# Keys, values and queries of layer B for two tiles at once, in three stages instead of five

## The reference

```
for layer in range(2):                                  # A = layer 0, B = layer 1
    shift/scale/gate rows = silu(c) @ ada_w[layer] + ada_b[layer]
    h = rmsnorm(x) * (1 + scale) + shift
    out = mla_mixer(h) if layer == 0 else band_mixer(h, k_all, v_all)
    x = x + gate_m * out
    x = x + gate_f * peer_ffn(rmsnorm-modulated x)
    if layer == 0:                                      # keys and values of layer B, from x after layer A
        k_new, v_new = h_kv @ w_kv ; k_new = rmsnorm per head(k_new)
# band_mixer: q = rmsnorm per head(h @ w_q); scores + relative bias, softmax, values; @ w_o
# peer_ffn: 8 heads choose 16 of 16384 experts for each row; for each chosen expert e:
#   a = gelu(h . u[e]);  y += softmax weight * a * v[e]        (u and v rows are 1024 floats)
```

## Time and profile before

| | |
|---|---|
| time, three runs | 4121.85, 4123.65, 4124.06 us |
| profiled execution: its own time, its span | 4123.38 us, 4121.6 us |
| mean granted clock of TensorE | 0.807 |
| busy: PE, DVE, POOL, ACT | 64%, 57%, 55%, 13% of the span |
| bytes moved | 1478 MB, mean 359 GB/s |
| of these by the gathers' queue q0, by SP's q1 | 1268 MB, 196 MB |

### The profile page before, as it was taken

How to read it: one execution, slowest core, us unless ns; L and a number is a source line. 1 busy time by engine, 2 the same in 40 slices (tenths; PEclk the granted TensorE clock), 3 DMA queues, 4 the chain that set the end, 5 groups by cost and what they waited for, 6 DMA issues and landing times.

```text
span 4121.6 us, 31777 instructions
## 1 busy us (share of the span) xinstructions
PE 2658.0 (64%) x9649; PEld 966.8 (23%) x9649; DVE 2330.6 (57%) x5876; ACT 527.1 (13%) x1288; POOL 2254.6 (55%) x2374
## 2 busy tenths in 40 slices
PE   6778664565554555555458567575656767676699
PEld 2344441221221112122112222132223211111122
DVE  2237687785676466556654655774576466544410
ACT  2244320111010101110011111011011100000000
POOL 1101436456666556565665555556566666666665
PEclk9889776777676786678679778777868899999999
DMA  9845988899999999999999999999999999999999
GB/s 344 306 162 167 306 269 324 303 340 371 381 395 390 387 412 380 386 363 415 390 390 381 401 379 352 387 365 392 406 408 403 371 361 356 370 371 369 377 373 341
DMA packets 480552, 1478.18 MB, mean 359 GB/s; under 512 B 59088, under 2 KB 132864, under 8 KB 479712
## 3 DMA queue, kind: packets, MB, share of 16 engines
q0 software_dynamic: 347792, 1268.25, 80.3%
q1 hardware_dynamic: 107008, 195.85, 12.9%
q10 hardware_dynamic: 25584, 12.06, 1.0%
HBM read 1448.97 MB, written 28.57 MB: 358 GB/s over the span
## 4 chain that ended last, share of the span: by engine, by line
DMA 28%; PE 19%; POOL 17%; DVE 14%; issue 13%; another core or an unknown queue 6%; ACT 2%; SPq 1%; ACTq 0%; DVEq 0%; POOLq 0%
DMA A<-in_uv,A 25%; POOL A L2049 9%; POOL A L2069 8%; PE P L997 8%; DVE A L1875 7%; PE P L939 2%; PE P L905 2%; PE P L715 1%; PE P L867 1%; PE P L652 1%; PE P L734 1%; DMA A<-in_w_oB 1%; DVE A L1761 1%; DVE A L1764 1%
## 5 line engine op out<-in xcount | busy, mean ns | idle before, releaser
L997 PE MATMUL P<-A 128*32 128x512 f32 x4608 | 1357.6, 819 | 1053.4 <-DMA A<-in_uv,A 909.8
L1875 DVE CUSTOM_DVE_ANT_0 A<-P,A 128x1024 f32<-128x1024 f32 x1052 | 1278.9, 1224 | 1048.3 <-DMA A<-in_uv,A 908.2
L2049 POOL DMA_INDIRECT A<-in_uv,A x1152 | 1112.4, 966 | 891.6 <-DVE A L1875 604.0
L2069 POOL DMA_INDIRECT A<-in_uv,A x1152 | 1096.6, 952 | 619.3 <-issue 295.2
L997 PEld LDWEIGHTS P<-A 128*32 128x32 f32 x4608 | 272.7, 133 | 1940.8 <-issue 1508.8
L1016 PE MATMUL P<-A 128*128 128x512 f32 (+1 forms) x480 | 230.6, 625 | 27.9 <-DMA A<-in_w_kv 18.6
L867 PE MATMUL P<-A 128*128 128x128 f32 (+2 forms) x832 | 150.7, 315 | 94.6 <-issue 48.8
L905 PE MATMUL P<-A 128*128 128x512 f32 (+1 forms) x320 | 171.1, 677 | 25.3 <-DMA A<-in_w_oB 17.6
L881 PE MATMUL P<-A 128*64 128x128 f32 (+2 forms) x832 | 137.6, 301 | 44.9 <-ACT A L1360 26.3
L854 PE MATMUL P<-A 96*64 96x320 f32 (+9 forms) x320 | 149.2, 575 | 18.9 <-issue 7.1
L867 PEld LDWEIGHTS P<-A 128*128 128x128 f32 (+2 forms) x832 | 119.4, 210 | 160.1 <-issue 112.6
(11 more groups left out here) (190 smaller groups left out, 2120.1 us busy)
## 6 DMA issues: line engine op xcount, KB each, us to landing
A<-in_ada_w POOLq DMA_DIRECT2D x28, 2048.0 KB, 10.9
A<-in_w_kv SPq DMA_DIRECT2D x80, 512.0 KB
A<-in_uv,A POOLq DMA_INDIRECT x2304
A<-in_w_oA SPq DMA_DIRECT2D x40, 512.0 KB
A<-in_w_q SPq DMA_DIRECT2D x40, 512.0 KB
A<-in_w_oB SPq DMA_DIRECT2D x40, 512.0 KB
A<-in_p_w_q SPq DMA_DIRECT2D x2, 4096.0 KB, 15.0
A<-in_p_w_q SPq DMA_DIRECT2D x8, 512.0 KB
```

The costliest lines, as they stand in the source:

```text
L997: ins = pe.matmul(Y[32 * j:32 * j + 32, b, :], spread[:, w:w + STRIDE], row[:, 512 * b:512 * b + 512], start=(m == 0), stop=(m == STRIDE - ...
L1875: dve.tensor_tensor_reduce(u_slot[b], row, u_slot[b], 1.0, 0.0, ALU.mult, ALU.add, dots[u % 2][:, j:j + 1]).then_inc(sem("dots_done"), 1)
L2049: pool.indirect_dma_start(u_slot[at % U_SLOTS], None, table, bass.IndirectOffsetOnAxis(ap=expert[u % 2][:, j:j + 1], axis=0)).then_inc(sem ...
L2069: pool.indirect_dma_start(row, None, table, bass.IndirectOffsetOnAxis(ap=expertT[u % 3][:, n:n + 1], axis=0)).then_inc(sem(name), 16)
```

## The change

- `MIDDLES = {3: (PT, 0), 5: (1, 2), 7: (3,)}`: the middle runs in stages 3, 5 and 7, for two tiles, two tiles and one. Stages 4 and 6 have none.
- A chunk of weights is multiplied with both tiles' rows before its slot is given back. Tile b uses banks 2b and 2b + 1, for all three products, so a product waits until the one before has been copied out.
- The ring has three chunks. Keys and queries share one pair of buffers; the second tile has `h` buffers of its own, one in place of a row buffer `hrow`, one in place of two bias strips.
- ACT copies keys and queries out of PSUM and squares them there; DVE scales the copies.
- PE pulls at m = 7 and 8 (turns of the two norms), four pieces at m = 9 to 12, 14 and 15, the turn of the keys at m = 13 and of the queries at m = 17; the attention from m = 19.
- SP writes keys and values in the midst of the queries' chunks, ahead of the 20th, since the queries need the keys' buffers.

```diff
+MIDDLES = {3: (PT, 0), 5: (1, 2), 7: (3,)}
...
-        mid_ring = [A[:, at:at + D] for at in (22560, 23584, 24608, 28448)]
-        vst = w_o[1]
-        kn_b, qn_b = A[:, 26144:27168], A[:, 27168:28192]
-        h_kv, h_q = oT, hT
+        first_ring = [A[:, at:at + D] for at in (22560, 23584, 24608, 28448)]
+        mid_ring = [A[:, 22560 + D * b:22560 + D * (b + 1)] for b in range(3)]
+        kn_b = qn_b = [A[:, 25632 + D * b:25632 + D * (b + 1)] for b in range(2)]
+        vst = [A[:, 27680 + D * b:27680 + D * (b + 1)] for b in range(2)]
+        h_kv, h_q = [oT, chunks(38688)], [hT, chunks(33568)]
...
-            return (m - 17) * 23 // 13 - (m - 18) * 23 // 13 if m >= 18 else 0
+            return (m - 18) * 23 // 12 - (m - 19) * 23 // 12 if m >= 19 else 0
...  SP, middle
+                def rows_stored():
+                    for b, t in enumerate(tiles):
+                        sp.wait_ge(sem("bk_normed"), done // 16 - len(tiles) + b + 1)
+                        load(o["bk_p"][rows_of(t), :] if t < PT else o["bk_s"][PAST - DEC:, :], kn_b[b][0:ROWS[t], :], "bk_stored")
+                    sp.wait_ge(sem("bv_copied"), i + 1)
+                    for b, t in enumerate(tiles):
...
+                sp.wait_ge(sem("out_chunks"), C * (stage + 2))
                 for x, (w, lo) in enumerate((("w_kv", 0), ("w_kv", D), ("w_q", 0))):
                     for c in range(C):
                         n = n0 + C * x + c
-                        if n - n0 >= 4:
-                            sp.wait_ge(sem("mid_chunks"), n - 3)
+                        if n - n0 >= 3:
+                            sp.wait_ge(sem("mid_chunks"), n - 2)
+                        if n - n0 == 19:
+                            rows_stored()
...  PE, middle
+                for b in range(2):
+                    if b < len(tiles):
+                        turn_norm("mid", tiles[b])
+                    yield
+                pe.wait_ge(sem("hT_ready"), norm_at["mid", tiles[-1]] + 1)
+                for x, (h, emptied) in enumerate(((h_kv, None), (h_kv, "bk_squared"), (h_q, "bkT_copied"))):
+                    if x == 2:
+                        turn_rows_back("bk", kn_b, "bv_copied", i)
+                        yield
+                    if emptied:
+                        pe.wait_ge(sem(emptied), i + 1)
                     for c in range(C):
                         n = n0 + C * x + c
+                        pe.wait_ge(sem(f"mid{n % 3}_loaded"), 16 * (C // 4 + n // 3 + 1))
+                        for b in range(len(tiles)):
+                            for half in range(2):
+                                ins = pe.matmul(P[:, 2 * b + half, :], h[b][:, c, :], mid_ring[n % 3][:, 512 * half:512 * half + 512],
+                                                start=(c == 0), stop=(c == C - 1), skip_group_check=True)
                         ins.then_inc(sem("mid_chunks"), 1)
                         yield
+                turn_rows_back("bq", qn_b, "bq_squared", i)
...  PE, the order of a stage
-                        if m in (7, 14, 16):
+                        if m in (7, 8, 13, 17):
                             pull(between)
-                        elif 8 <= m < 14:
+                        elif 9 <= m < 16:
                             pull(between, 4)
...  ACT
+                if u >= 2:
+                    act.wait_ge(sem("row_placed"), u - PLACED)
+                    act.wait_ge(sem("dots_done"), u_at(u - 1) + 4)
...
+            def middle_copies(i, x, rows, name):
+                tiles, squared = MIDDLES[list(MIDDLES)[i]], (xn, vst[1])
+                act.wait_ge(sem("mid_chunks"), 3 * C * i + (x + 1) * C)
+                for b in range(len(tiles)):
+                    for half in range(2):
+                        at = slice(512 * half, 512 * half + 512)
+                        ins = act.copy(rows[b][:, at], P[:, 2 * b + half, :])
+                        if name != "bv":
+                            ins = act.activation(squared[b][:, at], P[:, 2 * b + half, :], ACT.Square)
...
+                for name in ("bk_stored", "bv_stored", "vB_stored"):
+                    act.wait_ge(sem(name), 16 * done)
+                middle_copies(i, 2, qn_b, "bq")
...  DVE
+                for b in range(2):
+                    if b < n:
+                        if b == 0:
+                            dve.wait_ge(sem(f"{name}_rms"), i + 1)
+                            step(dve.reciprocal(stat[:, 64:64 + HEADS * n], stat[:, 64:64 + HEADS * n]))
+                        x = dst[b].rearrange("p (h e) -> p h e", h=HEADS)
+                        step(dve.tensor_tensor(x, x, bc(stat[:, 64 + HEADS * b:80 + HEADS * b].unsqueeze(2), [128, HEADS, BD]), ALU.mult))
+                        dve.tensor_tensor(x, x, bc(w.unsqueeze(1), [128, HEADS, BD]), ALU.mult).then_inc(sem(f"{name}_normed"), 1)
+                    yield
...
-                        elif e in (24, 47, 51, 63, 66):
+                        elif e in (24, 34, 51, 53, 55, 69, 71, 73):
                             pull(between)
```

More of the change, by code:

```diff
@@ L202, in build, with norm_bank @@
             norms.append((f"ffn{(stage + 1) // TILES}", ORDER[(stage + 1) % TILES]))
-            if MIDDLE <= stage < MIDDLE + TILES:
-                norms.append(("mid", ORDER[stage - MIDDLE]))
+            for t in MIDDLES.get(stage, ()):
+                norms.append(("mid", t))
         norm_at = {x: i for i, x in enumerate(norms)}
-        NORM_BANK = {"ffn0": 0, "mid": 0, "ffn1": 0}
+        second_mids = [tiles[1] for tiles in MIDDLES.values() if len(tiles) == 2]
+        def norm_bank(kind, t):
+            return 2 if kind == "mid" and t in second_mids else 0
         KEYS_A = [("past", 0), ("past", 1), ("new", PT)] + [("new", t) for t in range(PT)]
@@ L300, in has_middle, with middles_by, tiles_by @@
         def has_middle(stage):
-            return MIDDLE <= stage < MIDDLE + TILES
+            return stage in MIDDLES
+        def middles_by(stage):
+            return sum(s <= stage for s in MIDDLES)
+        def tiles_by(stage):
+            return sum(len(MIDDLES[s]) for s in MIDDLES if s <= stage)
         def pulls(stage, m):
@@ new lines, in middle @@
+                tiles, n0 = MIDDLES[stage], 3 * C * i
+                pe.wait_ge(sem("scores_copied"), stage + 2)
+                for b in range(2):
[9 more added lines that the diff above has]
+                        pe.wait_ge(sem(emptied), i + 1)
@@ L1023, in middle, with turn_rows_back @@
-                ins.then_inc(sem("bk_turned"), 1)
+                turn_rows_back("bq", qn_b, "bq_squared", i)
                 yield
-                pe.wait_ge(sem("bq_normed"), i + 1)
-                for c in range(C):
-                    ins = pe.transpose(P[:, c // 4, (c % 4) * 128:(c % 4) * 128 + r], qn_b[0:r, c * 128:(c + 1) * 128], ident[0:r, 0:r])
-                ins.then_inc(sem("bq_turned"), 1)
-                yield
+            def turn_rows_back(name, rows, emptied, i):
+                stage = list(MIDDLES)[i]
+                tiles = MIDDLES[stage]
+                pe.wait_ge(sem(emptied), i + 1)
+                for b in range(len(tiles)):
+                    pe.wait_ge(sem(f"{name}_normed"), tiles_by(stage) - len(tiles) + b + 1)
+                    for c in range(C):
+                        ins = pe.transpose(P[:, 2 * b + c // 4, (c % 4) * 128:(c % 4) * 128 + 128], rows[b][:, c * 128:(c + 1) * 128], ident[:, :])
+                ins.then_inc(sem(f"{name}_turned"), 1)
@@ new lines, in middle_rows @@
+                tiles = MIDDLES[stage]
+                if len(tiles) == 2:
+                    squares("mid", tiles[1])
+                for b, t in enumerate(tiles):
+                    act.wait_ge(sem("xn_turned"), norm_at["mid", t] + 1)
+                    act.wait_ge(sem("key_scores_ready"), stage + 2)
+                    modulate("kv", t, h_kv[b], 2 if t == PT else 1)
+                    modulate("mix1", t, h_q[b], 2 if t == PT else 1).then_inc(sem("hT_ready"), 1)
+            def middle_copies(i, x, rows, name):
+                tiles, squared = MIDDLES[list(MIDDLES)[i]], (xn, vst[1])
+                act.wait_ge(sem("mid_chunks"), 3 * C * i + (x + 1) * C)
+                for b in range(len(tiles)):
+                    for half in range(2):
[3 more added lines that the diff above has]
+                            ins = act.activation(squared[b][:, at], P[:, 2 * b + half, :], ACT.Square)
+                ins.then_inc(sem("bv_copied" if name == "bv" else f"{name}_squared"), 1)
@@ L1500, in project_rest, with middle_turns @@
+                middle_copies(i, 2, qn_b, "bq")
+                middle_rms(i, "bq")
+            def middle_turns(i, name, dst):
+                act.wait_ge(sem(f"{name}_turned"), i + 1)
+                for b in range(len(MIDDLES[list(MIDDLES)[i]])):
+                    for half in range(2):
```

(3 more changed lines are left out.)

165 lines of the change are left out of this document (59 added, 106 removed).

## The result

The changed kernel takes 4167.91 us (median of four, 4162.07 to 4182.41) against 4123.85 (4121.85 to 4128.58) of the kernel before: ratio 1.0109, 95% interval 1.009 to 1.0127. It is slower by 1.1%, 44 us; 15 us faster was forecast, and the time lies 29 us above the range. The profiled execution is the slowest of the four, 4182.41 us, so between the two profiles there are 59 us.

The account below looks back on a forecast made before the run. The prediction took DMA bytes to bound the kernel, with TensorE having little to spare in the weight stretches. Its terms, -73 + 12.6 + 3 + 24 + 15 + 3 = -15.4 us, gave 4108 us, range 4090 to 4125.

Parts of the forecast that it names:

- the 20th chunk's load is issued behind the stores: Stages 3 and 5: the load waits behind up to six stores in its queue, some 8 and 9 us.
- queue 1 has the engines for itself: At the queued stores: TensorE is late, so the gathers' slots are full, their queue empty, and the stores go unshared.
- rival B: Queued stores in stages 3 and 5 share engines with gathers, 20th chunk late by 18 and 25 us: 4139 us, chance 0.20.
- equal packets for each queue: DMA engines take packets in turn from the queues, whatever their size: 512-byte stores moved 0.50 MB against 3.58.
- The issues: SP's queue ahead of the 20th chunk: six store issues at 0.43 us each.
- its ring: Stage 7, three chunks instead of four: 6 waits of 3.2 us, mostly covered by TensorE's spare time, +3 us.
- The credit of the slots: Stages 3 and 5: gathers running ahead into 12 slots (15 us) hide 12 us of TensorE's lateness.
- the double work: Stages 3 and 5: two tiles' products make TensorE busy 102 and 105 us; +3 and +24 us after hiding.
- The bytes: Stages 4 and 6: 25.2 MB of chunk loads go and stores move away, -73 us; stores returning in 3 and 5, +12.6.
- Rival C: Stages 4 and 6 keep holes and gain 8 to 10 us less each, over 380 and 320: 4124 us, chance 0.12.
- The wait for the values' banks: Values' first chunk waits for ScalarE's 4 copies and 4 squares in the keys' banks: +2.5 us.
- Rival A: Gaps and slots hide TensorE's doubled products, stages stay bound by bytes, stage 5 under 335: 4066 us, chance 0.25.

Follow-up runs that it names:

- e14: Changed kernel with the queries in buffers of their own and SP's stores behind the 24th chunk, the kernel of e11 again: 3920.87 us, ratio 0.9924.
- e17: e14 with all six stores ahead of the 20th chunk, as in the changed kernel, nothing else different: 3968.41 us, ratio 1.0042.
- e5: The changed kernel, unaltered, run again on a slower chip than the first experiments': 4145.30 us, ratio 1.0084 to the kernel before.
- e3: Kernel before with only its three stores of keys and values moved ahead of the 20th chunk: 3961.99 us, ratio 1.0029.
- e1: Changed kernel with one tile in each of stages 3 to 7, so no bytes saved: 4017.20 us, ratio 1.0179.
- e4: Kernel before with a ring of three chunks in place of four, nothing else: 3953.83 us, ratio 1.0019.
- e6: The kernel before, unaltered, profiled on the same chip as e5: a single execution of 4126.76 us.
- e11: Changed kernel with the queries in buffers of their own and SP's stores behind the 24th chunk: 3919.66 us, ratio 0.9920.
- e15: e14 without the second tile's products with the weights in stages 3 and 5: 3913.31 us, ratio 0.9913.
- e16: e14 with the whole-row output stores ahead of the 20th chunk and the 512-byte pieces behind the 24th: 3947.16 us, ratio 0.9989.
- e2: Changed kernel with its six stores issued on ScalarE's queue after the copies of the turned keys: 3931.02 us, ratio 0.9962.

## Why the prediction was wrong, step by step

**The step that failed** is "the 20th chunk's load is issued behind the stores": "some 9 us in stage 5, 8 in stage 3", and nothing in stage 7. Measured, TensorE waits 18.25, 15.80 and 16.75 us in stages 3, 5 and 7, and the single edit of place (e14, e17) costs 47.5 us. Three things were off in it:
- "Against it: ... queue 1 has the engines for itself." It had not. In the 26 us up to the 20th chunk's use the gathers moved 5.65 MB. The clause was written against rival B and decided between it and the forecast. GpSimd had been held up by the slots before, but gathers issued as late as 2321.54 shared the engines with the stores. My own (equal packets for each queue, whatever their size) was the right row to go by, and it repeats here (544 and 536 packets). But it holds only until the gathers run dry: priced by it throughout, as in rival B, the chunk would be late by 25 us in stage 5, not 15.80.
- The issues: six at 0.43 us were counted, 2.6 in all. They took 11 us in stage 5 and 6.2 in stage 3, and three took 1.3 in stage 7; the 6.99 us are the issue of the second store in pieces. In the hole the engines moved 405 GB/s all the while, so how much of this is a cost of its own, no run separates.
- Stage 7 has three of the same stores ahead of its 20th chunk, and a single tile's chunks 18 and 19 cover 3.7 us of them where a pair's cover 7.4. The forecast looked only at its ring. That is the plainest miss: the loss of 28.9 us (17.6 in e5) in a stage whose work hardly changed.

**The credit of the slots.** "12 slots ... I take 12" us hidden. In e17 against e14 little of the holes is hidden: 3.1 of 18.3 us in stage 3, nothing in stage 5, 3.5 of 14.0 in stage 7. In the old order (e3) some three quarters are hidden. It would be natural to lay this to TensorE's time to spare, of which stages 3 and 5 have little (busy 101 of 107.8 and 98 of 104.9 us in e14's stretches). But stage 7 has one tile and time to spare (61 of 94.9) and still pays three quarters, and e1, with one tile in every stage, seems to pay all of it (56 us for 55.5 of waits against e4). That speaks for something in the new order of steps, and against the double work, as what makes the wait cost time. The old order has three steps of sums between the last product and the queries' turn and the new one two; that may be it, but no run changed it alone, and the cause of the two prices stays open.

**What the other steps measured.**

| step | forecast | first pair of profiles | e6 to e5 |
|---|---|---|---|
| bytes | -25.2 MB | -25.2 MB | |
| stage 4 | -36 us | -28.8 | -36.3 |
| stage 6 | -37 | -36.5 | -36.5 |
| stage 3 | +12 to +19 | +46.7 | +41.4 |
| stage 5 | +34 to +44 | +46.3 | +49.5 |
| stage 7 | +3 | +28.9 | +17.6 |
| TensorE busy in the stretches | 102, 105 | 100.8, 101.1 | |
| the same stretches' length | 118, 122 | 123.2, 123.2 | |

- The bytes pay in full, at some 36 us a stage; on the faster chips stages 4 and 6 take 348.9 and 293.1 us in e17 against 385.4 and 327.6 in e4. Only stage 4 of the first pair, 378.1 us, comes near C's mark of 380. Rival C falls.
- TensorE's double work is as summed, and so is the stretches' length, stage 5's to 1 us. The second is right by luck: in stage 5 the forecast's wait was 7 us too short and the terms around it 6 too long, since the stretch without the wait is 107.4 us (123.2 less 15.8) and mine without it was 113. The wait for the values' banks was 2.3 us in stage 3 (2.5 forecast).
- Stage 5 was forecast nearly right; of an error of 74 us in the first pair of profiles and 54 by the times of set 2 (+38.7 against -15.4), stage 3 holds 31 and 26, stage 7 26 and 15.
- Rival A (all hidden, stage 5 under 335) falls: e11, without the wait, has 349.0 there.
- Rival B is what happened, with three stages instead of two. It was given 0.20 and a price of 31 us, and said that it decides "once the extra wait is over 8 us in each of the two stages". The excess over the forecast's 8 and 9 was 10 and 7, just short of that in stage 5, with 17 in stage 7 beside it. My mark for it, a wait "of over 20 us", was set too high: 16 to 18 us were enough, since hardly any of it is hidden.
- The Trainium skill ("DMA: Bandwidth & Descriptors", section "Queues, rings and completion order") says that within a ring descriptors are consumed in order. e14 against e17 shows what that was worth here, 47.5 us: the rule that spoke against the change was the one to believe.

**What stays open.** From e14 (0.992) to the changed kernel (1.008 to 1.011) there are 1.6 to 1.9%, of which the place makes 1.2% in set 4. The rest is 17 to 28 us, and its cause is open. It isn't that the changed kernel's queries wait for the stores of the keys' buffers: in its trace ScalarE copies the queries within 0.2 us of their last product in stages 3 and 5. Nor does it look like SP's late issue in stage 3, 12.7 us after chunk 17 is done (5.8 in e5, and the cause is not known): e17 issues there after 0.2 us, and TensorE waits 18.0 us all the same. That the chips of set 4 and of the first comparison price the same place differently is left; e17 was not run on a slower chip. Stage 3 also has a wait of 23.8 us at its start, near the second norm, that no run took apart. And of the pair's 23 us in stage 5 only a part is known: products some 8 to 9 in stages 3 and 5 together (e15, not clear of noise), the rest the second norm, the turns and the write-back, not separated.

## What to carry to other kernels

A store that is moved ahead of a load in a queue costs its bytes and its issues to whoever waits for the load: count both against what covers that load, at the share of the engines that the other queues leave, in every stage that has the place, and look at what stands behind the waiting instruction. Saved bytes pay at the full rate where the stage is bound by them; work put together on one engine is paid as well. What a wait costs isn't told by the busy share of the engine that waits: here about a quarter of it in one order of the code, and three quarters to all of it in another, with one tile in a stage or two. When a change has a good and a bad part, find the bad one by a single edit: here two edits, behind the 24th chunk and buffers of their own for the queries, turn 1.1% slower into 0.8% faster (3919.66 and 3920.87 us, ratios 0.9920 and 0.9924).

## What was not expected of the hardware

- **Chips differ, and not by TensorE.** The kernel before takes 3948 to 3951 us in sets 1, 3 and 4, 4107 in set 2 and 4124 in the first comparison. In stages 8 and 9, with hardly more than gathers, the rate is 407 to 409 GB/s in the former (e14) and 362 to 372 in the latter, while 24 products of a pair take 10.57 us in both. Whether the same edit's ratio differs with it no run shows, so ratios are compared within a set.
- **Issuing a transfer takes as long as the queue makes it.** SP's issue of a store or load is 0.33 to 0.43 us as a rule; behind stores in 512-byte pieces one took 6.99 us in stage 5 (7.03 in e5, 7.40 in e17) and one 4.4 in stage 7. With only the large stores ahead (e16) none took more than 1.14 us at that place in stage 5.
- **Behind a hole the clock is lower.** In stage 5 the 8 products of the 20th chunk took 3.70 us at a granted clock of 1.00 (e14), 6.50 at 0.56 after the hole of 15.8 (changed kernel), 5.32 at 0.69 after 15.64 (e17), 5.13 at 0.72 after 10.59 (e16). In the last 8 us of the holes of the changed kernel and of e17 the clock had fallen to 0.50. The wait is thus paid a second time, by some 1.5 to 3 us. The length of the hole doesn't set the price: in e2 the same products took 5.40 us at 0.69 after a hole of 2.39.
